# Hybrid decoder block: the up projection's seven block products in seven banks, both halves of the activations in one 512-column product

## The reference

```python
up = rmsnorm(h, g_ffn[layer]) @ w_up[layer]              # 512 x 2048 times 2048 x 11264
up = causal_depthwise_conv(up, conv_w[layer], conv_b[layer])   # width 3
gate, val = jnp.split(up, 2, axis=-1)                    # 5632 channels each
h = h + (jax.nn.silu(gate) * val) @ w_down[layer]        # 5632 x 2048
```

## Time and profile before

| | |
|---|---|
| median of three runs | 2807.22 us (2806.18 to 2808.89) |
| the profiled execution, first to last instruction | 2806.6 us; no other time of it is shown |
| TensorE busy | 2798.6 us, 100% of the span |
| weight loads (PEld) busy | 2513.6 us, 90% |
| VectorE busy | 2087.2 us, 74% |
| ScalarE busy | 1248.4 us, 44% |
| GpSimd busy | 428.6 us, 15% |
| feed-forward stage | from about 1435 us to the end |

### The profile page before, as it was taken

One profiled execution on the slowest core, in us unless ns is written; L12 is line 12 of the kernel. 1 busy time (PEld: TensorE's weight loads), 2 busy tenths in 40 slices (PEclk: granted clock), 3 DMA queues, 4 the chain that ended last, 5 costly groups with the idle time before them and its releaser, 6 DMA issues.

```text
span 2806.6 us, 45334 instructions
## 1 busy us (share of the span) xinstructions
PE 2798.6 (100%) x16930; PEld 2513.6 (90%) x16930; DVE 2087.2 (74%) x3913; ACT 1248.4 (44%) x1701; POOL 428.6 (15%) x579
## 2 busy tenths in 40 slices
PE   9999999999999999999999999999999999999999
PEld 7788888888889999888899999999999999999998
DVE  7776677677777777444468987888788878887884
ACT  5444434433334334323355544444444444444543
POOL 1022154324400000001000111111111101110112
PEclk9999999999999999999999999999999999999999
DMA  5363586666534555444455655555555555565557
GB/s 177 137 184 94 176 193 132 177 186 128 113 115 157 175 168 176 147 134 150 142 170 145 142 136 136 134 138 137 137 133 139 136 135 136 136 137 137 136 137 165
DMA packets 187463, 411.24 MB, mean 147 GB/s; under 512 B 22288, under 2 KB 50320, under 8 KB 186128
## 3 DMA queue, kind: packets, MB, share of 16 engines
q1 hardware_dynamic: 120240, 283.90, 31.8%
q0 software_dynamic: 67040, 124.82, 23.7%
HBM read 347.81 MB, written 112.72 MB: 164 GB/s over the span
## 4 chain that ended last, share of the span: by engine, by line
PE 98%; DVE 1%; ACT 0%; DMA 0%; issue 0%; SPq 0%; DVEq 0%
PE bank L1852 12%; PE bank L1854 12%; PE bank L1853 12%; PE bank L2122 11%; PE bank L2124 11%; PE bank L2123 11%; PE bank L2157 6%; PE bank L2158 6%; PE bank L2159 6%; PE bank L2078 3%; PE bank L2079 3%; PE bank L2080 3%; PE bank L1926 1%; PE bank L1960 1%; PE bank L1971 0%; PE bank L1916 0%
## 5 line engine op out<-in xcount | busy, mean ns | idle before, releaser
L2122 PE MATMUL bank<-v_hi,w_hi 128*128 128x256 f32 x2464 | 697.6, 283 | 0.0
L2124 PE MATMUL bank<-v_hi,w_lo 128*128 128x256 f32 x2464 | 697.3, 283 | 0.0
L2123 PE MATMUL bank<-v_lo,w_hi 128*128 128x256 f32 x2464 | 697.3, 283 | 0.0
L937 ACT ACTIVATE w_hi<-w_raw 128x896 fp32r<-128x896 f32 (+1 forms) x528 | 444.9, 846 | 555.1 <-DVE w_raw L1648 384.4
L1655 DVE TENSOR_TENSOR w_lo<-w_raw,w_hi 128x896 fp32r<-128x896 f32 (+1 forms) x528 | 500.2, 953 | 126.9 <-ACT w_hi L937 126.0
L2122 PEld LDWEIGHTS bank<-v_hi,w_hi 128*128 128x128 f32 x2464 | 472.9, 192 | 2.0 <-issue 0.2
L2123 PEld LDWEIGHTS bank<-v_lo,w_hi 128*128 128x128 f32 x2464 | 472.9, 192 | 1.9 <-issue 0.2
L2124 PEld LDWEIGHTS bank<-v_hi,w_lo 128*128 128x128 f32 x2464 | 472.9, 192 | 0.0
L1852 PE MATMUL bank<-u_hi,w_hi 128*128 128x512 f32 x1000 | 396.2, 396 | 0.2 <-DVE w_lo L1078 0.2
L1854 PE MATMUL bank<-u_hi,w_lo 128*128 128x512 f32 x1000 | 390.5, 391 | 0.0
L1853 PE MATMUL bank<-u_lo,w_hi 128*128 128x512 f32 x1000 | 389.8, 390 | 0.0
(11 more groups left out here) (287 smaller groups left out, 4847.5 us busy)
## 6 DMA issues: line engine op xcount, KB each, us to landing
w_raw<-wslots SPq DMA_DIRECT2D x504, 256.0 KB, 2.7
w_raw<-wstream SPq DMA_DIRECT2D x189, 512.0 KB, 3.5
out_t<-stage POOLq DMA_DIRECT2D x168, 256.0 KB, 4.3
sums_scratch<-wfirst POOLq DMA_DIRECT2D x72, 448.0 KB, 5.7
g_raw<-sums_scratch SPq DMA_DIRECT2D x48, 448.0 KB, 3.2
g_raw<-wgates SPq DMA_DIRECT2D x48, 256.0 KB, 2.8
w_raw<-sums_scratch SPq DMA_DIRECT2D x24, 448.0 KB, 3.4
sums_scratch<-sums_scratch POOLq DMA_DIRECT2D x72, 128.0 KB, 4.7
```

Of the source, the lines that this page charges most:

```text
L937: act.activation(w4_hi[ring][:, 0:width], w4_raw[ring][:, 0:width], ACT.Copy).then_inc(w4_hi_ready, 1)
L2122: nc.tensor.matmul(out, wh, xh, start=kp == 0 and half == 0, stop=False, skip_group_check=True)
L2123: nc.tensor.matmul(out, wh, xl_, start=False, stop=False, skip_group_check=True)
L2124: ins = nc.tensor.matmul(out, wl, xh, start=False, stop=kp == KP - 1, skip_group_check=True)
```

## The change

For tiles f = 6 to 43 (38 of the 44), an up slot's product is one matmul of the high weights by high and low activations side by side (2 x 256 = 512 columns), and one of the low weights by the high activations (256 columns). `v_hi[kp]` and `v_lo[kp]` become the two halves of one tensor `v_parts[kp]`; the two pieces of 256 columns that one matmul reads lie 7 x 256 columns apart. The results need a whole bank per product (left half: high by high and low by high; right half: high by low), so seven banks, and the two halves are added after the slot's products: ScalarE copies the right halves to SBUF and VectorE adds the left halves, in two steps (products 0 to 2 while products 3 to 6 of the last slot still run, then products 3 to 6). `combine` and `take_up` then read SBUF. Down tiles use banks 7, 0, 1 and 7 in turn, so the copies out of them move: the third one of a tile from q = 2 of the next tile to q = 11, the fourth from q = 4 to q = 2. The copy of the right halves of products 0 to 2 stands ahead of `hi_slot(n + 3)` at q = 8 on ScalarE, and its addition ahead of `lo_slot(n + 2)` on VectorE. A few semaphores of the gate stage are merged with those of this stage; the waits stay the same.

The core of the diff:

```diff
+WIDE = 6
+WIDE_PRODUCTS = [(A11, B11), (S2, T2), (S3, T3), (A22, T4), (S1, T1), (A12, B21), (S4, B22)]
+EARLY = 3
...
+    def down_bank(d):
+        if d >= END:
+            return bank[2 + d % GROUP]
+        return bank[(7, 0, 1, 7)[d % GROUP] if wide(d // GROUP + 2) else GROUP + d % GROUP]
...
+            def low_halves(f, late):
+                if late:
+                    act.wait_ge(slot_done, START_F[f] + KP)
+                    act.wait_ge(s_raw_ready, f)
+                    act.activation(part_list(late_sum, 4), bank_halves(EARLY, 7, 1),
+                                   ACT.Copy).then_inc(low_copied, 1)
+                else:
+                    act.wait_ge(early_done, f - WIDE + 1)
+                    act.wait_ge(up_out, f - 1)
+                    act.activation(part_list(early_sum, EARLY), bank_halves(0, EARLY, 1),
+                                   ACT.Copy).then_inc(low_copied, 1)
...
-                if f > 2 and q in (2, 4):
+                if 2 < f < WIDE and q in (2, 4):
                     take_down(n, d0 - 2 + (q == 4), slots_done)
+                if f == WIDE and q == 0:
+                    take_down(n, d0 - 2, slots_done)
+                if f >= WIDE and q == 2:
+                    take_down(n, d0 - 1, slots_done)
...
                     if q == KP + 3:
+                        take_down(n, d0 + 2, slots_done)
                         conv_term(n, f, 1)
...
+            def add_halves(f, late):
+                k = 2 * (f - WIDE) + late
+                sums, j0, j1 = (late_sum, EARLY, 7) if late else (early_sum, 0, EARLY)
+                dve.wait_ge(low_copied, k + 1)
+                dve.tensor_tensor(part_list(sums, j1 - j0), bank_halves(j0, j1, 0), part_list(sums, j1 - j0),
+                                  ALU.add).then_inc(drained, 1)
...
             def combine(n, f):
+                if wide(f):
+                    add_halves(f, True)
+                    combine_wide(f)
+                    return
...
+            def bank_free(f, j):
+                d = GROUP * (f - 3)
+                if f == WIDE:
+                    if j >= GROUP:
+                        pe.wait_ge(down_out, GROUP + d + j - GROUP + 1)
+                    return
+                pe.wait_ge(drained, 2 * (f - WIDE) - (j < EARLY))
+                if j < 2:
+                    pe.wait_ge(down_out, GROUP + d + j + 2)
+
+            def wide_products(f, kp, ring):
+                for j, (w, x) in enumerate(WIDE_PRODUCTS):
+                    wh, wl = (t[ring][:, w * P:(w + 1) * P] for t in (w4_hi, w4_lo))
+                    both = v_parts[kp][:, :].rearrange("p (a c) -> p a c", a=2)[:, :, x * HALF:(x + 1) * HALF]
+                    if kp == 0:
+                        bank_free(f, j)
+                    nc.tensor.matmul(bank[j].rearrange("p (a c) -> p a c", a=2), wh, both, start=kp == 0, stop=False,
+                                     skip_group_check=True)
+                    ins = nc.tensor.matmul(bank[j][:, 0:HALF], wl, part(v_hi[kp], x), start=False,
+                                           stop=kp == KP - 1, skip_group_check=True)
+                    if kp == KP - 1 and j == EARLY - 1:
+                        ins.then_inc(early_done, 1)
+                return ins
```

More of the change, by code:

```diff
@@ L266, in build_program @@
     u_sum, v_sum, g_sum = sb("u_sum", HALF, 28 * K), sb("v_sum", HALF, 29 * K), sb("g_sum", SEQ, 30 * K)
+    early_sum, late_sum = sb("early_sum", 4 * HALF, 28 * K), sb("late_sum", 4 * HALF, tile[10] + 64)
     r_tok4 = sb("r_tok4", SEQ, 46 * K)
@@ L281, in build_program @@
     ntri, nones, nmask = (sb(n, P, tile[j]) for j, n in enumerate(("ntri", "nones", "nmask")))
-    bank = [nc.alloc_psum_tensor(f"bank{j}", [P, SEQ], F32) for j in range(8)]
+    banks = nc.alloc_psum_tensor("bank", [P, 8 * SEQ], F32)
+    bank = [banks[:, j * SEQ:(j + 1) * SEQ] for j in range(8)]
     Z = bank[2:6]
@@ L428, in part, with wide, bank_halves, part_list @@
         return t[:, j * HALF:(j + n) * HALF]
+    def wide(f):
+        return f >= WIDE
+    def bank_halves(j0, j1, half):
+        return banks[:, j0 * SEQ:j1 * SEQ].rearrange("p (b a c) -> p b a c", a=2, c=HALF)[:, :, half, :]
+    def part_list(t, n):
+        return t[:, 0:n * HALF].rearrange("p (b c) -> p b c", c=HALF)
+    def down_bank(d):
+        if d >= END:
+            return bank[2 + d % GROUP]
+        return bank[(7, 0, 1, 7)[d % GROUP] if wide(d // GROUP + 2) else GROUP + d % GROUP]
     with nc.Block() as block:
@@ L1008, in position @@
                 slots_done = place(n)[0]
+                if wide(f) and q == KP:
+                    low_halves(f, False)
+                hi_slot(n + 3)
                 d0 = GROUP * (f - 2)
@@ L1747, in position @@
             def position(n):
-                sums(n + 3)
-                lo_slot(n + 2)
                 at_ = n
@@ L1753, in position @@
                 q = at_ - START_F[f]
+                if wide(f) and q == KP:
+                    add_halves(f, False)
+                sums(n + 3)
+                lo_slot(n + 2)
                 if at_ == 0:
@@ L2105, in _, with down_free @@
                 unit3(KP - 1, p, p % 2, p // 2)
+            def bank_free(f, j):
[3 more added lines that the diff above has]
+                        pe.wait_ge(down_out, GROUP + d + j - GROUP + 1)
+                    return
+                pe.wait_ge(drained, 2 * (f - WIDE) - (j < EARLY))
[14 more added lines that the diff above has]
+                return ins
+            def down_free(d):
+                f, i = d // GROUP + 2, d % GROUP
+                if not wide(f):
+                    pe.wait_ge(down_out, d + 1)
+                elif d >= END + GROUP:
+                    pe.wait_ge(down_out, d + 1)
+                elif d >= END:
+                    pe.wait_ge(drained, 2 * (FT - WIDE))
+                elif i == 0:
+                    pe.wait_ge(down_out, GROUP + d)
+                elif i == 3:
+                    pe.wait_ge(down_out, GROUP + d - 2)
+                else:
+                    pe.wait_ge(drained, 2 * (f - WIDE) + 1)
             def up_slot(n):
@@ L2152, in down_slot @@
                         continue
-                    out = bank[GROUP + d % GROUP][:, :]
+                    out = down_bank(d)[:, :]
                     for f in fs:
```

72 lines of the change are left out of this document (49 added, 23 removed).

## The result

The kernel after takes 2836.64 us, the median of four runs (2835.53 to 2837.41); the kernel before, on the same chip, 2807.47 (2806.18 to 2808.89). The ratio is 1.0104, with a 95% interval of 1.0092 to 1.0115: **slower by 29.2 us**. The forecast was 2813.2 us, slower by 6.0, with a range up to 2834. So the direction was right, the size was not, and the range missed by 2.6 us.

A forecast was written before the change was run, and what follows sets the result against it. TensorE's matmul stream was taken as the bound: 2806.6 us of span, less 28.4 (Term 1), plus 34.4 (Term 3), made 2812.6, and 0.6 for the median of runs made 2813.2 us; range 2797 to 2834.

The forecast's parts named there:

- Term 3: Second product of tiles 7 to 43: TensorE waits for bank 1's copy, 0.93 us with restart, +34.4 us in all.
- Rival 2: Tile entrances: the third down copy is not late, so no gap; 2778.8 us, chance 0.07.
- Rival 4: Tile entrances: the stage buffer's DMA lands late, 0.5 us more per gap; 2831.7 us, chance 0.07.
- the covers: Slack for edits taken as free: bank 0's copy ends at T + 10.30, due at T + 10.91, 0.61 us left.
- Rival 6: Up-slot pairs: only a fifth of the fixed price goes with the dropped matmul, 5.7 us saved; 2835.9 us, chance 0.02.
- the skill's figure: Fixed price of about 2.5 ns per back-to-back matmul, by which dropping 2128 would save only 5.3 us.
- At the tail and at tile 6 old waits are met early.: At the tail and tile 6, claimed no new cost beyond waits already there; no time was added for it.
- Term 1: TensorE's up slots: a 512 and 256 pair takes 0.3467 us for 0.3600, saving 28.4 us over 38 tiles.
- rival 3: Up slots: the pair of 512 and 256 columns is dear, 0.351 us; 2822.4 us, chance 0.11.
- T: Start of a tile's first down matmul; the next up stretch starts at T + 10.91.

The follow-up runs named there:

- mended and sorted kernel: Kernel after, with ScalarE's down copies before `hi_slot`, wide form from tile 7, last tile's first down copy before `silu`, up-slot matmuls sorted by length: 2785.76 us.

## Why the prediction was right and wrong

**Right.** That the change would lose, and how. Term 3's gap is there at the second product of each of the 37 tiles, behind `hi_slot`, with every start within 0.03 us of the forecast; ScalarE's order alone removes it, and the length of one VectorE addition sets it one for one. Rival 2 (no gap) is out. Rival 4 (the stage buffer late at these entrances) came true in tile 31 alone, for 0.6 us; in the other 36 tiles ScalarE starts the copy without waiting for GpSimd. Of the covers, bank 0 held: no product 0 waits. Rival 6 and the skill's figure fall too: in the mended and sorted kernel a tile saves 20.15 - 19.54 = 0.61 us for 56 matmuls dropped, 0.0109 each with the borders' price inside it. The Trainium skill, "TensorE: Matmul & The Clock Gate", section "Wait — 56ns, not 53.3ns?", gives 0.0025; with a weight load before each matmul the runs here don't agree.

**Wrong, step by step.** The forecast was +6.0 of span, and +27.5 was measured; 21.5 are missing.

1. "At the tail and at tile 6 old waits are met early." This step failed, and cost 8.1 us at tile 6 (7.4 lost, 0.7 not saved) and 1.7 at the tail, nearly half of what is missing. I had read tile 5's copies only for their spacing of 0.39 us and took the steady tile, with its four down slots, for all. At tile 6 the banks just written are the ones that the new products want, the stretch behind is short, and the third copy waits for a stage buffer's DMA. The trace of before has the last of those three copies at 1588.71, where product 6 would want its bank at 1579.84 + 6 x 0.35 = 1581.94: it could be seen there and wasn't asked. On top came the clock, which fell to its 1.2 GHz level in the third of the waits, a cost for which the sum had no term. Starting at tile 7 takes all of it away.
2. Term 1, "I keep 0.3467", was mis-sized. The bounds held, 0.337 to 0.36, but in 23 of the 37 tiles the pair takes 0.353, in 14 it takes 0.3467. Over 56 pairs a dear tile loses 0.37 us: 23 x 0.37 = 8.5. This is rival 3 in 23 tiles (0.351 was its price) and the forecast in 14. The argument that the border only shifts the cost from one matmul to the next rested on one border each way; seven in a row gave another number.
3. Term 3's size: 1.04 us (38.7 in all, one gap of 1.7 among them) for 0.93. The copy ended within 0.03 us of the forecast; the restart was mis-sized. 0.05 became 0.14, while the first matmul's extra was 0.08 and not 0.11. The rest is 0.03 from the copy and 0.02 because the bank is due at T + 11.24, not 11.26., the only restart that I read, was another wait. With the late stage buffer of tile 31 this makes 4.3 us.

8.1 + 1.7 + 8.5 + 4.3 = 22.6; against it stand 1.3 us less ahead of tile 6, which no step of the change touches, and 0.4 in the down stretches: 20.9, and 0.6 us is left unassigned. Of the 1.3 us, 0.5 arise in the first 60 us of the two executions, and the rest where the one of the kernel before ran at a granted clock of 0.50 from 118.8 to 122.2 us and the one of the kernel after didn't.

**The range** took in the dear pair or the late buffer, but not both at once with a place that had been set to zero.

## What to carry to other kernels

When a change gives one engine new banks or buffers, ask for each of them who had it last, where that work's release stands in an in-order queue, and what the queue's head waits for; put releases that another engine waits for ahead of work that waits itself. Ask it again at the first and the last turn of the loop, where the stretch behind has another length, since waits there can also come with a fall of the clock. And once the waits are gone, group matmuls of one length: with the order and the grouping mended, this change, a loss of 1.0%, is a gain of 0.8%.

## What the runs showed of the hardware

- Matmuls of 512 and 256 columns in turn ran at one of two prices, 0.3467 or 0.353 us per pair, the same through a whole up stretch, and without a change in the code between tiles. A tile's 20.45 and 20.8 us in the windows of the kernel after are these two. What selects between them is open; it isn't chance alone, for in the kernel after the order from tile 7 on is dear, dear, cheap, six times over.
- Seven matmuls of 512 columns whose moving operand lies in two pieces, 7 x 256 columns apart, took 1.59 us, as much as seven in one piece at their even 0.2266.
- Outside the cheap alternating form, which costs no more than the two even prices together (0.3467), a change of length has its own small price: per slot 2.47 us with seven changes to and fro, 2.44 with one, and 19.48 against 19.54 us per tile when half of these go too.
- In tile 6 the granted clock stayed at 1.00 through waits of 1.66 and 0.37 us, fell to 0.50 some 0.7 us into the next one, and the first 4.0 us of matmuls behind it ran at the 1.2 GHz level. In the 37 tiles with a gap of 1.04 us the clock stayed at 1.00. The length of one wait doesn't settle it: a wait of 2.7 us some 115 us into the kernel was followed by 0.50 from 118.8 to 122.2 us in the profiled execution of the kernel before, and by no fall in that of the kernel after.
- TensorE's restart after a wait for ScalarE's copy took 0.14 us from the copy's shown end in the 37 gaps and in the tail, and 0.05 us (1586.81 after 1586.76) at the three waits of tile 6. In the code the former matmuls have another semaphore wait directly ahead of the one for the copy, the latter don't; that this makes the difference was not tested. The first 512 columns took 0.31 us instead of 0.23.
